# Down weights of the narrow expert blocks in 8 KB rows, and their hidden tile turned by four 64-column products

## What is computed

```python
def swiglu(x, w_gate, w_up, w_down):
    return (jax.nn.silu(x @ w_gate) * (x @ w_up)) @ w_down

# moe_ffn: N_EXPERTS = 64, TOP_K = 6, D_EXPERT = 256, dm = 1024, all float32
affinity = jax.nn.sigmoid((h @ router_w).astype(f32))
_, idx = lax.top_k(affinity + router_bias.astype(f32), TOP_K)
...
def expert_block(acc, blk):
    tok, g, e = blk
    y = swiglu(h_ext[tok], w_gate[e], w_up[e], w_down[e])
    return acc.at[tok].add(y * g[:, None]), None
...
return acc[:n_tok] + swiglu(h, ws_gate, ws_up, ws_down)
```

## Time and profile before

| | us |
|---|---|
| median of 3 runs | 2556.77 (2554.54 to 2557.51) |
| the profiled execution, its own time | 2554.8 |
| its span, first to last instruction | 2553.0 |
| TensorE busy in the span | 2150.4 |
| VectorE busy | 905.5 |
| ScalarE busy | 616.9 |
| GpSimd busy | 454.3 |

### The profile page before, as it was taken

The page is one execution under the profiler, slowest core; times in us unless marked ns, Lnnn a source line. Parts: engine busy times, 40 slices in busy tenths (PEclk is TensorE's granted clock), DMA queues, the critical chain, the costliest instruction groups (busy, mean ns, idle before and its releaser), DMA issues. The chain is left out here.

```text
span 2553.0 us, 39589 instructions
## 1 busy us (share of the span) xinstructions
PE 2150.4 (84%) x11733; PEld 1189.5 (47%) x11734; DVE 905.5 (35%) x2012; ACT 616.9 (24%) x1079; POOL 454.3 (18%) x423
## 2 busy tenths in 40 slices
PE   5889999896999999999999527399789999987883
PEld 4665445744444444444444316164444444444442
DVE  8844375934412111111111257932421111111113
ACT  3443233602122121112121124030221222211110
POOL 1000000002112222222222211200122222232231
PEclk9999999998999999999999858699899999999997
DMA  9970102004699999999998687940399999899995
GB/s 358 382 263 33 45 22 82 1 1 184 278 332 360 353 355 363 353 358 351 354 363 285 193 277 234 251 160 0 145 378 374 354 362 357 279 380 370 390 377 186
DMA packets 167668, 672.72 MB, mean 263 GB/s; under 512 B 37858, under 2 KB 40898, under 8 KB 123546
## 3 DMA queue, kind: packets, MB, share of 16 engines
q1 hardware_dynamic: 116650, 577.23, 59.0%
q0 software_dynamic: 38208, 69.04, 11.3%
q10 hardware_dynamic: 12720, 25.27, 2.6%
HBM read 622.28 MB, written 89.24 MB: 279 GB/s over the span
## 5 line engine op out<-in xcount | busy, mean ns | idle before, releaser
L1431 PE MATMUL banks_l<-slotw_l,xTw_l 128*128 128x512 f32 x800 | 357.9, 600 | 24.9 <-issue 24.9
L1442 PE MATMUL banks_l<-slotn_l,xTn_l 128*64 128x256 f32 x2816 | 328.2, 386 | 33.9 <-issue 33.9
L1442 PEld LDWEIGHTS banks_l<-slotn_l,xTn_l 128*64 128x64 f32 x2816 | 213.5, 138 | 180.0 <-issue 105.3
L1431 PEld LDWEIGHTS banks_l<-slotw_l,xTw_l 128*128 128x128 f32 x800 | 148.5, 190 | 236.2 <-issue 236.2
L1481 PE MATMUL banks_l<-slotn_l,late_l 128*64 128x512 f32 x704 | 189.9, 615 | 18.4 <-DVE late_l L1283 16.6
L1460 PE MATMUL banks_l<-slotw_l,late_l 128*128 128x512 f32 x400 | 191.8, 602 | 15.4 <-DVE late_l L1269 15.4
L946 POOL DMA_INDIRECT xgw_l<-moe_h,idxw_l x58 | 60.7, 1047 | 768.6 <-PE banks_l L1376 634.9
L974 POOL DMA_INDIRECT moe_acc<-late_l,idxn_l x88 | 141.2, 1604 | 192.6 <-DMA moe_acc<-late_l,idxn_l 174.2
L1266 DVE TENSOR_TENSOR late_l<-late_l,banks_l 128x256 f32<-128x256 f32 x50 | 21.1, 421 | 340.9 <-ACT late_l L1072 340.9
L1231 DVE TENSOR_TENSOR onehotn_l<-iota_slot_l,rank_l 128x512 bf16 (+1 forms) x98 | 79.4, 811 | 133.9 <-issue 133.9
L556 PE MATMUL ps_a<-W_a,hT_a 128*128 128x512 f32 x288 | 124.8, 595 | 0.0
(11 more groups left out here) (402 smaller groups left out, 3058.9 us busy)
## 6 DMA issues: line engine op xcount, KB each, us to landing
slotn_l<-in_exp_w_gate SPq DMA_DIRECT2D x88, 1024.0 KB
slotn_l<-in_exp_w_up SPq DMA_DIRECT2D x88, 1024.0 KB
slotn_l<-in_exp_w_down SPq DMA_DIRECT2D x88, 1024.0 KB, 11.7
slotw_l<-in_exp_w_gate SPq DMA_DIRECT2D x50, 1024.0 KB
slotw_l<-in_exp_w_up SPq DMA_DIRECT2D x50, 1024.0 KB
slotw_l<-in_exp_w_down SPq DMA_DIRECT2D x50, 1024.0 KB
w_p<-in_mod_w SPq DMA_DIRECT2D x12, 2048.0 KB, 15.2
W_a<-in_ar_w_in SPq DMA_DIRECT2D x5, 2048.0 KB, 9.2
```

What stands on the lines that cost most here:

```text
L1431: last = pe.matmul(pGU_w, xT_w[b % 2][:, k, :], wgu[0][b % WIDE_RING][:, :, k, :], start=(k == 0), stop=(k == KD - 1))
L1442: last = pe.matmul(pGU_n[H * side:H * side + H, b % 2], xT_n[b % 2][:, k % 4, H * (k // 4):H * (k // 4) + H], w[:, :, k, P * side:P * side ...
```

## The change

The down weights of narrow blocks are loaded like those of wide ones: partition p gets features 2p and 2p + 1 in one run of 8 KB. Side 0 holds features 0 to 127, so these are now at partitions 0 to 63, and side 1's at partitions 64 to 127. The turn has to bring them there. It becomes four products (k = 0, 1 and side = 0, 1), each with every second column of `hid_n` as the stationary operand (128 partitions x 64 columns) and the 64 columns of the identity that pick one side as the moving one (64 columns). Each writes 64 partitions and 64 columns of `pHT`. Nothing else is touched; lines after L861 move by one, and after L1471 by four more.

```diff
             def load_down(kind, slot, i):
                 e = expert(sp, kind, i)
-                rows = ("e (p k) n -> p (e k) n", "e (k p) n -> p (e k) n")[kind]
-                sp.dma_start(wd[kind][slot], w_down[bass.ds(e, 1)].rearrange(rows, k=2))\
+                sp.dma_start(wd[kind][slot], w_down[bass.ds(e, 1)].rearrange("e (p k) n -> p (e k) n", k=2))\
                   .then_inc(d_loaded[kind][slot], 16)
@@
             def rest_narrow(i, q, b):
                 pe.wait_ge(N['hid_done'], i + 2)
-                pe.transpose(pHT[:, 0, :], hid_n, ident[:]).then_inc(N['hidT_mm'], 1)
+                for k in range(2):
+                    for side in range(2):
+                        at = slice(H * side, H * side + H)
+                        last = pe.matmul(pHT[at, 0, H * k:H * k + H], hid_n.rearrange("p (c k) -> p k c", k=2)[:, k], ident[:, at],
+                                         start=True, stop=True, skip_group_check=True)
+                last.then_inc(N['hidT_mm'], 1)
```

## The result

The changed kernel takes **2577.0 us** (median of 6 runs, 2572.3 to 2581.4). The kernel before, run beside it, takes 2556.8 (2554.5 to 2557.5). The ratio is 1.008, 95% interval 1.0066 to 1.0094. It is slower by 20 us; the forecast was 2573.0 with a range of 2558 to 2592. The profiled execution took 2579.9 us for a span of 2578.2, so its span is 25.2 us longer than that of the kernel before (2553.0). The experiments' kernels are compared with the kernel before as it ran beside them: 2557.6 (first set), 2558.1 (second), 2556.1 (third).

What follows compares the result with a forecast made beforehand. TensorE was taken to bound the pairs, the scatters' landing the narrow blocks alone. 2554.8 + 2.2 + 4.9 + 1.4 + 7.8 = 2571.1, with 2.0 for the runs' median: 2573 us, range 2558 to 2592.

Steps and rivals of the forecast that it cites:

- What bounds the kernel: Expert stages: TensorE bounds the pairs; with narrow blocks alone the scatters' landing sets the pace, 9.17 us per step.
- Layer 0's pairs: Turn in layer 0's pairs: 0.47 us more, mostly hidden by the wait before L1481; 12 x 0.18 = 2.2 us.
- Layer 1's pairs: Turn in layer 1's pairs: 0.47 us more in 16 turns, less a wait of 2.7 us; 4.9 us comes through.
- The products' row: The four new products on TensorE: eight passes of 64 columns take 0.45 us, as in the mixer's row.
- The turn alone: Narrow blocks alone: turn 0.2 us longer, absorbed while weights flow, counted in seven blocks; 1.4 us.
- The scatter: Layer 1's narrow blocks alone: scatters delayed beside 8 KB rows by 0.25 us per block, 31 x 0.25 = 7.8 us.
- How many rows a scatter has: Scatter of narrow blocks: 128 rows, 8 for each of 16 engines, giving an upper end of 1.2 us per block.
- The rule on queues: DMA engines change queue only after a packet of 9 to 17 descriptors; scatter term 0, sum 2563.3.
- 1, scatters don't move: Narrow blocks alone: scatters land as before, only TensorE's terms count; 2565 us, chance 0.33.
- 2, a full 8 KB row for each scattered row: Narrow blocks alone: each scattered row waits behind an 8 KB row, 37 us more; 2602 us, chance 0.10.
- 3, TensorE's price hidden: Turn: passes pulled ahead under L1460, mode costs nothing, scatters stay; 2557 to 2560 us, chance 0.15.
- 4, the scatter lands sooner: Narrow blocks alone: fewer queued rows let scatters start earlier; 2554 us, up to 2547 without pair losses, chance 0.07.

Runs made afterwards that it cites:

- rows_only: The changed kernel with the single transpose put back, so 8 KB rows for narrow down weights and TensorE as before: 2567.2 us, ratio 1.0035.
- products_twice: The kernel before with its transpose as four products of 64 columns, each issued twice (eight products): 2580.2 us, ratio 1.0087.
- rows_layer1: The kernel before with 8 KB rows for the narrow down weights in layer 1 alone, single transpose in both layers: 2571.8 us, ratio 1.005.
- products_only: The kernel before, 4 KB rows kept, with its transpose written as four products of 64 columns: 2562.9 us, ratio 1.0035.

## Why the prediction was right, point by point

- **What bounds the kernel.** Right in both regimes. In the pairs no gap appeared before the gate and up products, faster loads brought nothing (`rows_only`, layer 0: 660.4 against 660.3), and TensorE's added work counts. Alone, the chain of scatters sets the pace: take it away and 8 KB rows cost nothing that can be seen.
- **Layer 0's pairs, 2.2 us.** For the 32 turns of the table that is 2.1. Measured 1.4 with the products alone, 0.9 and 1.2 in the two traces of the changed kernel against the first of the kernel before. The wait took in what it was said to, and a little more.
- **Layer 1's pairs, 4.9 us.** Measured 4.0 with the products alone, 5.3 and 4.1 in the changed kernel, over 15 turns. The first of them varies by the run; the other 14 took 3.5, 3.6 and 3.6 us more (0.25 each, 0.31 forecast). The down product starts 1.12 us after the turn's first product; 1.2 was forecast.
- **The products' row, 0.45 us.** It reads 0.46. What it stands for was misread: the prediction needs it for one group alone, but as a rate of 0.45 per four products, as the expectation for `products_twice` took it, it fails, since four more cost 0.25. The forecast's total for a turn nearly held, presumably because the mixer's row holds the same fixed part.
- **The turn alone, 1.4 us for seven unloaded turns.** Layer 0's four, with the last pair, cost 0.6 against 0.8 forecast; layer 1's 31 loaded turns took nothing (324.1 with the products alone). Once the scatters' delay was gone, the products were next, as said: 319.4 against 314.3.
- **The scatter, 0.25 per block, 7.8 us.** The direction and the chain were right, the size too small, and its working had a wrong premise. The landing rose from 8.2 and 8.4 us in the two traces of the kernel before to 8.7 and 8.8 (8.4 to 8.5 forecast), the step by 0.33 and 0.36: from 9.18 to 9.51, and to 9.54 in the second trace. The whole stage grew by 8.7 and 11.0 us, where the forecast has 8.4 (7.8 and the last three turns' 0.6).
- **How many rows a scatter has.** The prediction counts 128, eight for each of 16 engines. But a narrow block is seldom full: token numbers out of range are skipped (`bounds_check`), and the trace's packet records have 16 to 128 packets of 2 KB per scatter in this stage, 65 in the mean (2016 for 31 scatters from 2213 to 2495). That is four for each engine, so the upper end, one row of weights let ahead by each scattered row, is 4 x 0.15 = 0.6 us per block and not 1.2 (an estimate from these counts and the prediction's rates). The measured 0.33 and 0.36 are over half of it, and `rows_layer1`, with 9.71 - 9.18 = 0.53, comes near it, where the prediction took a fifth of its own upper end: "most of the eight rows find few of these rows left". So twice the rows and too small a share of them nearly cancelled, and that 0.25 came out close is partly luck. That each scattered row does wait behind a row of weights fits these numbers; the order inside an engine isn't shown.
- **The rule on queues.** By the Trainium skill ("DMA: Bandwidth & Descriptors", section "Queues, rings and completion order") an engine changes queue after a packet of many descriptors, which made the scatter's term 0. The runs speak against that as the measure of the wait here: with the number of bytes kept, down rows of 8 KB gave landings of 8.7 to 8.9 us and down rows of 4 KB 8.2 to 8.4, and with gate and up rows of 4 KB as well GpSimd hardly waited. No trace here shows the engines' own switching.
- **The sum.** Forecast 16.3 us for the expert stages. The changed kernel's two traces give 15.5 and 16.9 against the first trace of the kernel before. The other 3 to 5 us to the measured 20 lie before and between the expert stages, where the prediction had no term and the runs vary by several us.
- **The rivals.** 1, scatters don't move: `rows_layer1`, ratio 1.005, refutes it. 2, a full 8 KB row for each scattered row: its 37 us are three times what was measured and its sign, a landing of 9 us or more, wasn't met (8.7 to 8.9), so its price is ruled out. Its mechanism is not ruled out: with 65 rows instead of 128 it would be some 19 us (31 x 0.6), against 10 to 11 by the changed kernel's steps and 16 by those of `rows_layer1`. 3, TensorE's price hidden: `products_only`, 1.0035, refutes it. 4, the scatter lands sooner: it lands later. By the rivals' own chances the three outcomes add up to 0.78, 0.18 and 0.04 rather than 0.79, 0.15 and 0.06.

## What to carry to other kernels

A transfer that others wait for can pay for the size of its neighbours' rows: here larger rows of weights moved at a rate that nothing needed, and delayed the scatter that everything waited for. Count the rows that a data-dependent transfer really moves before pricing it by its full size. A DMA share of 1.01 doesn't say that bytes are the bound; ask for whom the next issue waits, and free that wait first: here it brought 12 us, and left the row size without effect. Before costing a reordering step by a row of the trace, ask how much of the row is its start and how much its rate, since only the second part grows with the count.

## What the runs showed of the hardware

- Four float32 products of 64 columns read 0.46 us as a group, eight 0.69: about half of the 0.46 doesn't grow with the count.
- While weights flow, over half of a scatter's landing passes before its first row moves: the first 2 KB packet starts 4.7 us after the issue (median, kernel before) of the 8.2, and 2.2 us after it once the loads have stopped.
- A float32 moving operand read at a step of 8 bytes slows TensorE by 5% (3.85 against 3.67 us for 32 passes of 256 columns), not by half.
- Scatters that did not wait for one another did not slow the loads beside them: the stage moved 385 GB/s instead of 376.
- Down rows in two transfers of 2 KB rows were slower than one of 4 KB (ratio 1.0042), and layer 0's pairs lost 3.3 us too; why wasn't found.
